# Work moved beside the input projection, and attention's operand splits reordered, in a four-layer kernel

## The reference

```python
mod = (c_act @ w_ada[l] + b_ada[l])[:, None, :]
sh_m, sc_m, g_m, sh_f, sc_f, g_f = jnp.split(mod, 6, axis=-1)
h = x * (1.0 + sc_m) + sh_m
(aq, ak, av, iq, ik, iw, rq, rk, rv, rg, mq, mk, mv, mo, mi, mf) = jnp.split(h @ w_in, SPLIT_POINTS, axis=-1)
# index: iq (4 heads of 64) and ik (1 head) are rotated; iw weighs the 4 heads; the top 128 keys of each query are kept
o_a = dsa_attention(rope(aq), rope(ak), av, rope(iq), rope(ik), iw)      # 8 heads of 64, softmax over the kept keys
o_b = head_norm(retention(rope(rq), rope(rk), rv)) * silu(rg)
qk = silu(causal_conv(concat([mq, mk])))
o_c = head_norm(sigmoid(mo) * mlstm(qk, mv, mi + i_bias, mf + f_bias))  # gates: 4 rows mi, 4 rows mf
x = layer_norm(ALPHA * x + (1 + g_m) * (concat([o_a, o_b, o_c]) @ w_out))
# then a mixture of experts with a second norm
```

## Time and profile before

| | us |
|---|---|
| median of 3 runs | 3868.04 (3867.3 to 3870.64) |
| the profiled execution, its own time | 3864.45 |
| its span in the trace | 3862.7 |
| w_in of layer 0, from its first to its last work | 37.7 to 252.0 |
| index_weights and rope_index of layer 0 | 252.0 to 262.5 |
| sparse_attention of layer 0 | 349.5 to 418.5 |
| mlstm_opening of layer 0 | 418.5 to 440.8 |
| w_in of layer 1 | 942.2 to 1139.8 |
| band_attention (16 heads) | 3240 to 3376 |

### The profile page before, as it was taken

How to read it: one execution, slowest core, us unless ns; L and a number is a source line. 1 busy time by engine, 2 the same in 40 slices (tenths; PEclk the granted TensorE clock), 3 DMA queues, 4 the chain that set the end, 5 groups by cost and what they waited for, 6 DMA issues and landing times. The chain is left out here.

```text
span 3862.7 us, 43362 instructions
## 1 busy us (share of the span) xinstructions
PE 3343.2 (87%) x16972; PEld 2709.8 (70%) x16972; DVE 2297.0 (59%) x3573; ACT 1318.6 (34%) x1866; POOL 630.8 (16%) x548
## 2 busy tenths in 40 slices
PE   8976778997996787998994888879999897699998
PEld 7763567886872566886763876767778787577787
DVE  7868646995658645996645663554442433644534
ACT  2123524772122623774312111123232324632222
POOL 0025501000006501000502341301100102511000
PEclk8986788999996787999996997889999998899999
DMA  7620004991530002992220000002222221022222
GB/s 277 239 88 0 1 17 158 375 375 72 207 120 0 1 20 84 374 375 114 87 82 11 1 1 1 1 12 104 77 94 93 86 90 48 28 93 87 88 98 77
DMA packets 59578, 401.33 MB, mean 104 GB/s; under 512 B 6768, under 2 KB 8432, under 8 KB 12272
## 3 DMA queue, kind: packets, MB, share of 16 engines
q1 hardware_dynamic: 53616, 356.62, 25.0%
q0 software_dynamic: 5760, 41.95, 3.0%
HBM read 396.45 MB, written 2.10 MB: 103 GB/s over the span
## 5 line engine op out<-in xcount | busy, mean ns | idle before, releaser
L135 PE MATMUL ps<-t_part,weight_hi 128*128 128x512 f32 x2152 | 863.4, 401 | 69.9 <-DVE scr_part L180 38.4
L137 PE MATMUL ps<-t_part,ring_lo 128*128 128x512 f32 x2152 | 851.4, 396 | 0.0
L136 PE MATMUL ps<-scr_part,weight_hi 128*128 128x512 f32 x1640 | 650.4, 397 | 0.0
L347 DVE TENSOR_TENSOR ring_lo<-ring,weight_hi 128x2048 fp32r<-128x2048 f32 x133 | 311.1, 2339 | 386.7 <-ACT weight_hi L340 386.7
L135 PEld LDWEIGHTS ps<-t_part,weight_hi 128*128 128x128 f32 x2152 | 413.5, 192 | 163.6 <-DVE ring_lo L167 69.7
L340 ACT CAST weight_hi<-ring 128x2048 fp32r<-128x2048 f32 x133 | 253.7, 1907 | 667.6 <-PE ps L137 667.6
L137 PEld LDWEIGHTS ps<-t_part,ring_lo 128*128 128x128 f32 x2152 | 412.0, 191 | 87.9
L136 PEld LDWEIGHTS ps<-scr_part,weight_hi 128*128 128x128 f32 x1640 | 316.9, 193 | 69.2 <-issue 3.9
L136 PE MATMUL ps<-big_part,weight_hi 128*128 128x512 f32 x512 | 200.3, 391 | 0.0
L201 POOL TENSOR_TENSOR big<-big 128x512 f32<-128x512 f32 x28 | 47.9, 1709 | 891.7 <-ACT big L194 888.2
L449 DVE SCALAR_TENSOR_TENSOR scr_q<-t,c_act,scr_q 128x256 f32<-128x256 f32 x294 | 142.6, 485 | 10.5
(11 more groups left out here) (613 smaller groups left out, 7222.9 us busy)
## 6 DMA issues: line engine op xcount, KB each, us to landing
ring<-in_w_moe SPq DMA_DIRECT2D x84, 1024.0 KB, 5.1
t<-in_w_moe SPq DMA_DIRECT2D x84, 1024.0 KB, 4.9
ring<-in_w SPq DMA_DIRECT2D x64, 1024.0 KB, 4.8
t<-in_w_ada POOLq DMA_DIRECT2D x40, 1024.0 KB, 5.2
ring<-in_w_in SPq DMA_DIRECT2D x32, 1024.0 KB, 5.9
ring<-in_even_in SPq DMA_DIRECT2D x15, 1024.0 KB, 4.8
ring<-in_qkv SPq DMA_DIRECT2D x12, 1024.0 KB, 4.8
ring<-in_w_out SPq DMA_DIRECT2D x8, 1024.0 KB, 4.8
```

The costliest lines, as they stand in the source:

```text
L135: pe.matmul(bank, w_hi, x_hi, start=first, stop=False)
L136: pe.matmul(bank, w_hi, x_lo, start=False, stop=False)
L137: return pe.matmul(bank, w_lo, x_hi, start=False, stop=last)
L347: v.tensor_tensor(K.ring_lo[:, g % NSLOT, :], K.ring[:, g % NSLOT, :], K.w_hi[:, n % 2, :].bitcast(F32), ALU.subtract).then_inc(w_lo.up(), 1)
```

## The change

1. **The weighed columns.** Layer 0 weighs two columns in steps 0 to 9 (as before) and one in each of steps 10 to 13; none is left for 14 and 15. Layer 1 has all its 16 within steps 0 to 9. The first 20 are weighed into eight places in odd tiles of `big` (25 to 31) instead of two, and PE sums them behind step n+2 of their step n; the last four keep the two places in `scr_q` and are summed behind step n+1.
2. **Rotation and gates.** A new class `MixerBeside` does the index rotation and the gate rows within w_in: PE's three swaps behind steps 8, 10 and 12, POOL's cos products behind the loads 19, 22 and 23, DVE's part in steps 9, 11 and 13; the gate rows in steps 12 and 14; the transposes of gate rows and index weights behind step 15. The stages `index_weights` and `rope_index` are gone. The layout of `w_in` puts the index weights beside the gate rows.
3. **mlstm_opening** loses the gate rows; the keys' `lo` parts go from POOL to DVE.
4. **Attention.** The keys' `hi` part comes behind the second item's exponentials (ACT) and its `lo` behind the third item's normalisation (POOL); the queries' `lo` comes behind the fourth item's normalisation. PE waits for the queries' `lo` only ahead of the third matmul.

```diff
@@ linear
-    ada = AdaBeside(K, side, len(steps), 10, 14) if side else None
+    ada = AdaBeside(K, side, len(steps)) if side else None
...
             if ada:
-                ada.sum(pe, n - 1)
+                ada.sum(pe, n)
             if beside:
                 beside.pe(pe, n)
-        if ada:
-            ada.sum(pe, len(steps) - 1)
...
-        if conv:
-            conv[3](v)
-        if ada:
-            ada.bias(v)
+            if conv and n == 14:
+                conv[3](v)
+            if ada and n == 14:
+                ada.bias(v)
...
-        for i in range(len(side or ())):
-            ada.load(g, i)
+        for i in range(24 if ada else 0):
+            if i < len(side):
+                ada.load(g, i)
+            if beside:
+                beside.g(g, i)
@@ AdaBeside
+        first = min(len(columns), 20)
+        self.until = [-(-first * min(n + 1, 10) // 10) + max(0, min(n - 9, len(columns) - first)) for n in range(nstep)]
+        odd = lambda i: K.big(25 + 2 * (i // 2 % 4))[:, (i % 2) * BC:(i % 2 + 1) * BC]
+        self.part = lambda i: odd(i) if i < 20 else K.scr_q[:, (i % 2) * BC:(i % 2 + 1) * BC]
...
     def sum(self, pe, n):
-        for i in self.of_step(n):
-            ada_sum(self.K, pe, self.columns[i][2], i, self.done, i + 1)
+        for i in [*self.of_step(n - 2), *self.of_step(n - 1)]:
+            if i < 20 and i in self.of_step(n - 2) or i >= 20 and i in self.of_step(n - 1):
+                ada_sum(self.K, pe, self.columns[i][2], i, self.done, i + 1, self.part(i))
@@ softmax_attention
             if t == 0:
-                pe.wait_ge(ql.sem, ql.at(prepared(h)))
+                pe.wait_ge(qh.sem, qh.at(prepared(h)))
+                pe.wait_ge(ql.sem, ql.at(prepared(h) - 1))
...
+            if t == 0:
+                pe.wait_ge(ql.sem, ql.at(prepared(h)))
             pe.matmul(bank(n)[:, 0:w], q_lo, k_hi(h // 2)[:, 0:w], start=False, stop=True).then_inc(sc.up(), 1)
...
+        def keys_lo(h):
+            g.wait_ge(qh.sem, qh.at(prepared(h) - 1))
+            g.tensor_tensor(k(h // 2)[1], k(h // 2)[0], k_hi(h // 2).bitcast(F32), ALU.subtract).then_inc(ql.up(), 1)
...
-            if n % ST == 1 and n // ST + 2 < heads:
-                operands_lo(n // ST + 2)
+            if n % ST == 2 and n // ST % 2 == 0 and n // ST + 2 < heads:
+                keys_lo(n // ST + 2)
+            if n % ST == 3 and n // ST + 2 < heads:
+                queries_lo(n // ST + 2)
...
+                if n % ST == 1 and n // ST % 2 == 0 and n // ST + 2 < heads:
+                    keys_hi(n // ST + 2)
                 if n % ST == 3 and n // ST + 2 < heads:
-                    operands_hi(n // ST + 2)
+                    queries_hi(n // ST + 2)
@@ mlstm_opening, vector and gpsimd
+        for h in range(4):
+            v.wait_ge(oh.sem, oh.at(2 + h + 1))
+            r = parts.rows(h)
+            v.tensor_tensor(parts.k(h, 1)[r, :], parts.k_raw(h), parts.k(h, 0)[r, :].bitcast(F32), ALU.subtract).then_inc(st.up(), 1)
...
-            g.tensor_tensor(parts.k(h, 1)[r, :], parts.k_raw(h), parts.k(h, 0)[r, :].bitcast(F32), ALU.subtract).then_inc(lo.up(), 1)
@@ MixerBeside (new)
+    def pe(self, pe, n):
+        if n in (8, 10, 12):
+            i = (8, 10, 12).index(n)
...
+            if i >= 1:
+                pe.wait_ge(self.rotated.sem, self.rotated.at(i))
+            pe.matmul(K.ps[:, 6, :], K.swap[:, :], self.chunks[i], start=True, stop=True).then_inc(self.swapped.up(), 1)
+        if n == 15:
+            pe.wait_ge(self.rotated.sem, self.rotated.at(3))
+            pe.wait_ge(self.hv.sem, self.hv.at(3))
...
+    def v(self, v, n):
...
+        if n in (9, 11, 13):
...
+            do(v.tensor_tensor(t, K.ps[:, 6, :], K.sin[:, :], ALU.mult))
+            v.wait_ge(self.scaled.sem, self.scaled.at(i + 1))
+            v.tensor_tensor(c, c, t, ALU.add).then_inc(self.rotated.up(), 1)
```

More of the change, by code:

```diff
@@ L429, in g_, with ada_part @@
             rms.add(g)
-        if beside:
+        if beside and not ada:
             beside.g(g)
-        for i in range(len(side or ())):
-            ada.load(g, i)
+        for i in range(24 if ada else 0):
[3 more added lines that the diff above has]
+                beside.g(g, i)
     K.stage(name, tensor=pe_, vector=v_, scalar=s_, **({"gpsimd": g_} if ada or rms or beside else {}),
             **({"sync": beside.sync} if beside else {}))
-def ada_part(K, v, w, i, done):
+def ada_part(K, v, w, i, done, part, ring=2):
     step, summed = K.sig("v_step"), K.sig("ada_summed")
-    part = K.scr_q[:, (i % 2) * BC:(i % 2 + 1) * BC]
-    if i >= 2:
-        v.wait_ge(summed.sem, summed.at(i - 1))
+    if i >= ring:
+        v.wait_ge(summed.sem, summed.at(i - ring + 1))
     v.tensor_scalar(part, w[:, 0, :], K.c_act[:, 0:1], None, ALU.mult).then_inc(step.up(), 1)
@@ L450, in ada_part, with ada_sum @@
         ins.then_inc(*((step.up(), 1) if k < 7 else (done.up(), 1)))
-def ada_sum(K, pe, b, i, done, count):
+def ada_sum(K, pe, b, i, done, count, whole):
     summed = K.sig("ada_summed")
@@ L457, in ada_sum @@
     for half in range(2):
-        part = K.scr_q[:, (i % 2) * BC + half * P:(i % 2) * BC + (half + 1) * P]
+        part = whole[:, half * P:(half + 1) * P]
         ins = pe.matmul(K.ps[:, 7, 2 * b + half:2 * b + half + 1], part, K.ones[:, 0:1], start=True, stop=True)
@@ L587, in v_ @@
             v.wait_ge(ld_w[b].sem, ld_w[b].at(16))
-            ada_part(K, v, block(b), i, done)
+            ada_part(K, v, block(b), i, done, K.scr_q[:, (i % 2) * BC:(i % 2 + 1) * BC])
         m, bias = K.mod[:, 0, 0:16], K.vec("b_ada", 0)[:, 0:16]
@@ L1275, in g_ @@
             g.tensor_tensor(parts.values(t, 1), parts.v_raw(t), parts.values(t, 0).bitcast(F32), ALU.subtract).then_inc(lo.up(), 1)
-        g.wait_ge(lo.sem, lo.n)
-        g.wait_ge(gated.sem, gated.at(2))
-        for h in range(4):
-            g.wait_ge(oh.sem, oh.at(2 + h + 1))
-            r = parts.rows(h)
-            g.tensor_tensor(parts.k(h, 1)[r, :], parts.k_raw(h), parts.k(h, 0)[r, :].bitcast(F32), ALU.subtract).then_inc(lo.up(), 1)
-    def s_(s):
-        step = K.sig("s_step")
-        s.wait_ge(hv.sem, hv.at(1))
-        s.activation(R(0, 32), R(0, 32), ACT.Exp, scale=-1.0).then_inc(step.up(), 1)
-        s.wait_ge(step.sem, step.n)
-        s.activation(R(0, 32), R(0, 32), ACT.Ln, bias=1.0).then_inc(hs.up(), 1)
+    def s_(s):
         for c in range(2):
@@ L1330, in spread @@
                 pe.wait_ge(nm.sem, nm.at(h))
-            one_hot = K.ident[0:4, h:h + 1].to_broadcast([4, P])
-            pe.matmul(K.ps[:, 6, :], one_hot, K.scr[0:4, 3 * S:4 * S], start=True, stop=True).then_inc(bc.up(), 1)
+            one_hot = K.ident[32:36, 32 + h:33 + h].to_broadcast([4, P])
+            pe.matmul(K.ps[:, 6, :], one_hot, K.big(23)[32:36, :], start=True, stop=True).then_inc(bc.up(), 1)
         def score(n):
@@ L2194, in first_layer @@
     columns = [(0, b) for b in range(8, 24)] + [(1, b) for b in range(8)] if l == 0 else [(1, b) for b in range(8, 24)]
-    first = {}
+    first = {"beside": MixerBeside(K, Angles(K, a) if l == 0 else None)}
     if l == 0:
@@ L2244, in first_layer @@
     parts = MlstmParts(K, vt)
-    mlstm_opening(K, big(23), parts, lambda c: K.t2(4 + c), lambda c: big(14 + c))
+    mlstm_opening(K, parts, lambda c: K.t2(4 + c), lambda c: big(14 + c))
     mlstm(K, parts, lambda h: K.t2(6 + h // 2)[rows(h), :], lambda c: big(20 + c))
```

187 lines of the change are left out of this document (96 added, 91 removed).

## The result

The changed kernel takes 3776.66 us (median of 4 runs, 3773.38 to 3778.81), the kernel before 3869.34 (4 runs, 3867.30 to 3871.49): a ratio of 0.976 (0.9743 to 0.9777). In five more runs beside a later group of experiments it took 3770.66 (3769.41 to 3777.43), ratio 0.9747 (0.9734 to 0.976). Forecast were 3773 and a range of 3758 to 3795. The profiled execution took 3777.16 us; its span is 3775.4 for 3862.7 before, 87.3 us less.

The account below looks back on a forecast made before the run. It took w_in as PE-bound with holes from the sums' wait, and attention as held by a wait made by order. Savings of 27.8, 14.6, 7.6, 43.0 and 1.6 sum to 94.6; 3868.0 less that gives 3773 us, range 3758 to 3795.

Parts of the forecast that it names:

- w_in, layer 0: Layer 0's w_in up to the index stage: index stage starts at 234.7 in place of 262.54, saving 27.8 us.
- the sum: All the stages' forecast savings added, 94.6 us, taken from 3868.0 to give 3773.
- w_in, layer 1: Layer 1's w_in up to the index stage: it ends at 1135.6 in place of 1150.18, saving 14.6 us.
- Swaps at full clock and the short tail: In w_in: three swaps on PE's path take 2.6 us, and transposes, copy, exponential and hand-over behind it 2.6.
- The rival that DVE still sets the pace: In w_in: DVE still limits the steps; half of 21.4 us stays, giving 3784; chance 0.12.
- mlstm_opening: POOL's last group of 5.67 us goes; less 0.6 and 1.3 this saves 3.8 per opening, 7.6 us for both.
- The charge of 0.6 for the port: In mlstm_opening: POOL loses 0.6 us through DVE working on the keys beside it.
- The table load: The exponential table's load, 1.28 us, moves into mlstm ahead of its first exponential and lies on the path.
- Attention: Heads return to 5.50 us plus ACT's splits, saving 8.8, 8.8 and 25.4, together 43.0 us, plus 1.6 at starts.
- The wait made by order: In attention: POOL idles 2.83 us, standing behind the second item for what ACT makes behind the fourth.
- The rival of splits that stay on the path: In attention: ACT cannot absorb the splits, so 17.3 us less is saved, giving 3790; chance 0.15.
- the one that the stall changes its name: In attention: PE waits for the queries' part at the next head's scores, taking back 44.6, giving 3818; chance 0.04.

Follow-up runs that it names:

- e4: The changed kernel with columns 20 and 21 of w_ada waiting for no sum: 3764.41 us, ratio 0.9734 to the kernel before (changed kernel beside it 3770.66).
- e5: The changed kernel with the keys' low part in mlstm_opening back on POOL, behind the values: 3783.79 us, ratio 0.9787 to the kernel before.
- e6: The changed kernel with one more one-column exponential ending ACT's work in mlstm_opening, loading the table there: 3770.97 us, ratio 0.9751 to the kernel before.
- e3: The kernel before with POOL's low parts of a later head's operands behind the fourth normalisation, not the second: 3833.50 us, ratio 0.9907.
- e8: The changed kernel with PE taking a stage's mean of squares (L209) behind step 1's last product, not its first: 3761.34 us, ratio 0.9725 to the kernel before.
- e2: The changed kernel with attention as it was before: 3818.09 us, ratio 0.9864 to the kernel before.
- e1: The kernel before with only the attention part of the change: 3828.51 us, ratio 0.9901.
- e7: The changed kernel with mlstm_opening's own work on ACT, DVE and POOL in another order: 3776.24 us, ratio 0.9751 to the kernel before.
- e9: The changed kernel with all weighed columns in two scr_q places, summed one step behind their weighing: 3793.65 us, ratio 0.9803 to the kernel before.
- e11: The kernel before with PE taking a stage's mean of squares behind the last product of step 1: 3861.60 us, ratio 0.9971.

## Why the prediction was right, and where its terms were not

**w_in, layer 0: the mechanism right, 6.6 us too much.** From step 1 to the index stage the sum had 170.8 us; it took 176.2. What failed is the sentence "DVE has one column (4.0), the convolution (about 3) and a rotation or gate piece (1.5) in place of two columns, so it fits 11.5": it counted DVE's work and not what that work waits for. In the changed kernel `ring` goes to 2 at column 20, and the wait for column 18's sum comes with it. e4 takes it away and measures 170.8 (67.05 to 237.89), the sum's number. The other 1.2 of the 6.6 lie between w_in's first matmul and the end of step 1 (24.7 us for 23.5 before; it is 23.4 to 25.0 in the traces of the changed kernel and its variants, with no order by the edits).

**w_in, layer 1: right.** 14.7 for 14.6; with 16 columns no column uses scr_q, so the wait does not exist there. Swaps at full clock and the short tail were priced rightly: in layer 0 a step with a swap takes 12.68 us for 11.83, three times 0.85 for the 2.6 of the sum, and the index stage starts 2.2 us behind w_in's last matmul, for 2.6. The rival that DVE still sets the pace would have left half of 21.4 us in w_in; in e4 nothing is left of it.

**mlstm_opening: 6.2 and 6.0 for 5.1, with the wrong shares.** The forecast gave everything to POOL's last group (5.7 less 0.6). e5 gives 2.8 of it to the keys' move at the same clock (that is the low one, or nearly, in both layers of both profiles). The other 3.1 to 3.4 us come, by subtraction, from the gates. With their scans and short instructions on DVE, POOL's values took 5.05 us; with DVE idle in e5 they take 2.76. That the whole of the 3 us is this hold, and not the gates' own length on DVE, is not shown. The charge of 0.6 for the port was too small: 4.57 - 2.76 = 1.8 is what POOL pays for DVE's four keys. The 2.8 that the prediction worked out as the hold on POOL from the Trainium skill (SBUF — State Buffer, Who interferes with whom) missed the 1.8 by less than the 0.6 that I went by. The rows after the change show the hold on both sides: DVE's four take 4.63 for 2.8 alone. It did not lower the sum, since the same hold had been there before the change.

**The table load: wrong, 1.3 us an opening.** It is in mlstm as forecast (408.50, 1.28 us), and e6 shows that it costs nothing: PE has other matmuls up to its next spread of a row, which does not move. The 2.66 us that the Trainium skill (ScalarE: Activation LUTs, What ACT_TABLE_LOAD costs) gives for load and drain do not show here either: the load takes 1.28, and the exponential starts at 409.80, 0.02 us behind its end.

**Attention: right.** 9.9 and 9.8 for 9.6, and 24.0 for 25.4 in the band. Heads of 5.51 and 5.96 us answer to 5.50 and 5.82: in the band the keys' split costs a head 0.46, not 0.32, and in the two short attentions 0.28 (5.78). ACT is busy for 5.53 of the 5.96 us. POOL's load was counted too low: the prediction took 0.64 us for the queries' part, which no row shows; it takes 1.28 (3228.41). An even head's POOL work is then 2.85 + 1.28 + 1.28 = 5.4 and not 4.8, not under 90% of 5.5. It did no harm, since over two heads POOL is busy for 9.4 of 11.47 us. The wait made by order was the right reading, and e3 shows it with one number. The rival of splits that stay on the path (6.1 each head) falls, as does the one that the stall changes its name. Layer 0's five heads take 29.7 us (347.17 to 376.86) for the 28.1 of the sum; 1.1 of it is the first head, 7.41 us where the band's is 6.3.

**Not in the sum at all:** 4.2 us behind the band and 2.1 at the start. e8 shows that 3.2 of the first are PE's wait at L209 with its clock, for without the wait that stage gives 4.7 us back. The other 1.0 is the clock in a later stage, read from rows alone. Whether the change brings the long wait on is open: the eight traces with the new order of attention and L209 in its old place all have it behind the band, and the kernel before, e2 and e3 do not; but near 1780 us the kernel before and the changed one both have the short wait and e1 and e7 the long one. The start is chance: w_in's first matmul stands at 42.52 and 42.28 in two runs of the changed kernel, at 42.11 in e4, and at 40.45 in the kernel before and 39.86 in e9, with the same code ahead of it; e3 and e11, the kernel before with one line changed further on, have 42.19 and 42.92. In sum, 6.6 + 1.4 (band) + 4.2 + 2.1 = 14.3 too much, and 2.0 (openings), 4.5 (mlstm and behind it), 0.5 (short attentions) and 0.1 too little: 94.6 - 14.3 + 7.1 = 87.4, the 87.3 of the spans but for rounding. Of the 4.5, 2.6 are the table load that cost nothing twice; the other 1.9 lie in stages that the change does not touch.

## What to carry to other kernels

Before pricing what an engine does in a step, write down every wait that the step's instructions carry and what stands behind it on the other engine; a ring's size that changes on the way (8, then 2) made waits for places that nobody held. An instruction in the wrong place of POOL's queue, an engine with time to spare, cost a quarter of the band's attention, and moving one number gave 34.5 of the 39.5 us of that edit: try such a move alone first. A gain of a few us can be lost in a later stage, as e7's was, so look at the first long wait of the busiest engine in every stage behind it. And compare a stage with itself only at the same clock: mlstm_opening differs by 1.8 us by that alone.

## What the runs showed of the hardware

- At L209 behind the band the wait has two sizes, and the clock mostly follows. Waits of 1.49 to 1.50 us (before, e2, e3) left it at 2.4 GHz; waits of 2.61 to 2.90 (the changed kernel twice, e1, e4, e5, e7, e9) were followed by matmuls of 0.63 us, 1.2 GHz. But e6 waited 2.90 as well and kept 2.4 GHz. Near 3020 us even waits of 1.95 to 2.05 (L208) were followed by 1.2 GHz in every trace that has them, and so was e9's of 1.50 there. So a stage to whose mean PE comes 1.4 us sooner can give 3 to 4 us back, and no row here says surely when. PE's timeline of e6:

```profile
3353.49 1.13 PE L209 MATMUL ps<-big,mean_d 128*128 128x512 f32 x2 [2.90 <-POOL big L201]
3354.06 0.80 PE L135 MATMUL ps<-t_part,weight_hi 128*128 128x512 f32 x1
3354.69 0.40 PE L136 MATMUL ps<-scr_part,weight_hi 128*128 128x512 f32 x1
```
- POOL and DVE hold each other, both ways: POOL's 128x256 subtraction takes 0.69 us alone and 1.14 beside DVE's, DVE's 64x512 one 0.70 (e7, POOL idle) and 1.16. Their four instructions each start in turn (DVE at 399.56, 400.82, 401.96, 403.09; POOL at 400.21, 401.34, 402.48, 403.60), and each side takes 1.8 us longer.
- The 2.1 us by which w_in starts later are PE's clock. The same 32 matmuls of the first stage take 4.33 us in the profile before and 6.96 in the one after, and the granted clock from 30 to 35 us is 0.81 and 0.50:

```profile
30.21 4.33 PE L537 MATMUL ps<-c_act,big 128*128 128x1 f32 x32
```

```profile
29.63 6.96 PE L543 MATMUL ps<-c_act,big 128*128 128x1 f32 x32
```
